# The low part of one weight unit, made later in VectorE's order

## The chip, the cores and the metric

One core of a Trainium2 chip runs the whole kernel. The metric is the device time of one execution in microseconds (us); three runs of the kernel before gave 766.83, 767.84 and 767.82 us, median 767.82.

## The reference

A two-layer decoder trunk on 256 tokens with 1024 features, in float32. Layer one is a stick-breaking attention with 16 heads of 64; layer two is a dilated windowed attention that reads a shared K/V. Each layer ends in a SwiGLU feed-forward. The change lies in layer one, at the end of its attention:

```python
z = jnp.einsum('bhqd,bhkd->bhqk', q_blk, kf) * scale
log_stay = jnp.where(strict, jax.nn.log_sigmoid(-z), 0.0)
log_a = jax.nn.log_sigmoid(z) + lax.cumsum(after, axis=3, reverse=True)   # after: log_stay moved on by one
a = jnp.where(strict, jnp.exp(log_a), 0.0)
o = jnp.einsum('bhqk,bhkd->bhqd', a, vf)      # all heads, then  o @ w_o
```

## The kernel before

Every engine has its own list of instructions, written out by hand, and runs it in that order; semaphores join the lists. No planner places anything: an instruction stands where the program puts it.

**Weights.** They pass through in units, numbered in one row over the whole program. A unit is loaded by SyncE's queue into one of three buffers `raw` (number modulo 3), its high part is made by ScalarE (`hi(s)`, line 511) and its low part, raw minus high, by VectorE (`lo(s)`, line 800), into six buffers `w_hi` and `w_lo`. TensorE then makes three matmuls for each product (high by high, high by low, low by high). The load of unit s waits for the low part of unit s - 3 (`sp.wait_ge(lo_made, ...)` in `load`), the high part for the landing, the low part for the high part. Units 20 and 21 are the query and key weights of head pair 7, the last one, of 1024 columns each. Units 22 to 25 are the four units of the first output projection (`WOA0` = 22), of 2048 columns; units 26 on are the feed-forward.

**Attention of layer one** goes by eight pairs of heads, 0 to 7. For a pair, VectorE takes the projected queries and keys out of PSUM (`take_qk_a`, lines 921 and 922); TensorE makes the scores (`scores_a`, lines 1252 and 1253); ScalarE makes three steps of a softplus (lines 579, 581, 583; the last signals `ell_made`); VectorE's `scores_a` makes four instructions (lines 900, 902, 903, 905) with ScalarE's line 593 between them; TensorE sums over the keys (`sums_a`, line 1285); VectorE subtracts that (`stay_a`, line 912); ScalarE's exponential (line 596) and VectorE's mask (`mask_a`, line 917) give the weights; TensorE multiplies them with the values (`outputs_a`, lines 1297 and 1299); VectorE cuts the output in two (`outputs_a`, lines 882 and 884). The pairs are staggered: while one pair is in its sums, the next one's projections run on TensorE.

**Around the change**, TensorE's list is: projections of pair 7 (lines 1197 to 1199, units 20 and 21), `sums_a(6)`, `scores_a(7)`, output projection by unit 22 and the first half of unit 23 (`out_proj`, lines 1191 to 1193), `outputs_a(6)`, more of it, `sums_a(7)`, unit 24, `outputs_a(7)`, the rest. VectorE's list is: take pair 6, stay 5, lo(20), mask 5, lo(21), lo(22), outputs 5, scores 6, take pair 7, stay 6, lo(23), mask 6, scores 7, outputs 6, lo(24), stay 7, lo(25), mask 7. SyncE's list there is: the load of unit 25 (which waits for lo(22)), four loads of x into `xn`, the load of unit 26 (which waits for lo(23)).

TensorE's `scores_a(7)` waits for `qka_made`, which the second instruction of `take_qk_a(7)` sends.

Of the kernel before, what the change touches and what calls it, by code (L numbers as in the profile page):

```python
# [34 lines left out]
PAIRS = NH // 2  # L35
# [26 lines left out]
WOA0 = A0 + 3 * PAIRS  # L62
# [39 lines left out]
def build(nc, x, norm_gains, w_qkv_a, w_o_a, g_kv, w_kv_b, w_q_b, w_o_b, rel_bias, w_gate_up, w_down,  # L102
# [16 lines left out]
    with ExitStack() as ctx:  # L119
# [94 lines left out]
        def bank(b, lo=0, n=512):  # L214
            return ps[:, 512 * b + lo:512 * b + lo + n]
# [5 lines left out]
        def banks(b, m, n):  # L221
            return ps[:, 512 * b:512 * (b + m)].rearrange("p (m n) -> p m n", m=m)[:, :, 0:n]
# [46 lines left out]
        def query_a(p):  # L269

            return A0 + (3 * p + 1 if p else 0)
# [5 lines left out]
        def size(s):  # L277
            return KT * P if s < WOA0 else 4 * NG * P if B0 <= s < WOB0 else UNIT
# [517 lines left out]
        def _(dve):  # L796
            def lo(s, j=0):
                dve.wait_ge(hi_made, j * 6 + s + 1)
                n, c = size(s), s % CUT
                dve.tensor_tensor(w_lo[:, c, 0:n], raw[:, s % RAW, 0:n], w_hi[:, c, 0:n].bitcast(F32), ALU.subtract  # L800
                                  ).then_inc(lo_made, 1)
# [84 lines left out]
            def outputs_a(a, j):  # L886

                dve.wait_ge(pva_done, j * 2 + a + 1)
                cut_ot(j * 2 + a, bank(7, 0, SEQ).rearrange("p (t m r) -> p t r m", t=NT, r=R), j * 2 + a + 1)

            def diagonals(buf):

                return buf.rearrange("p h (b n) -> p h b n", n=P)[:, :, 0:3:2, :]
# [3 lines left out]
            def scores_a(a, j):  # L897
                z = banks(3, 2, WA)
                dve.wait_ge(ell_made, j * 2 + a + 1)
                dve.scalar_tensor_tensor(spl, z, 0.0, ell, ALU.max, ALU.add).then_inc(spl_made, 1)  # L900
                dve.wait_ge(spl_made, j * 2 + a + 1)
                dve.tensor_tensor(diagonals(spl), diagonals(spl), strict4, ALU.mult).then_inc(spl_masked, 1)
                dve.scalar_tensor_tensor(arg, z, 0.0, ell, ALU.min, ALU.subtract).then_inc(arg_made, 1)
                dve.wait_ge(spl_hi, j * 2 + a + 1)
                dve.tensor_tensor(spl_cut[1], spl, spl_cut[0].bitcast(F32), ALU.subtract).then_inc(spl_cut_made, 1)

            def stay_a(a, j):
                dve.wait_ge(arg_made, j * 2 + a + 1)
                dve.wait_ge(r_done, j * 2 + a + 1)
                for lo_, n, b in ((0, SEQ, 5), (SEQ, P, 6)):  # L910
                    part = arg[:, :, lo_:lo_ + n]
                    inst = dve.tensor_tensor(part, part, two_heads(b, n), ALU.subtract)
                inst.then_inc(stay_made, 1)

            def mask_a(a, j):
                dve.wait_ge(wts_made, j * 2 + a + 1)
                dve.tensor_tensor(diagonals(wts), diagonals(wts), strict4, ALU.mult).then_inc(wts_masked, 1)

            def take_qk_a(p, j):
                dve.wait_ge(*((w_used, j * 6 + query_a(p) + 2) if p else (first_used, 2)))  # L920
                dve.scalar_tensor_tensor(qa, bank(0, 0, SEQ), SCALE, rows[:, :], ALU.mult, ALU.mult)
                dve.tensor_tensor(ka, bank(0, SEQ, SEQ), rows[:, :], ALU.mult).then_inc(qka_made, 1)

            def step_a(p, j):
                s = A0 + 3 * p + 4
                if p >= 2:
                    outputs_a(p - 2, j)
                scores_a(p - 1, j)
                take_qk_a(p, j)
                stay_a(p - 1, j)  # L930
                lo(s, j)
                mask_a(p - 1, j)
                lo(s + 1, j)
                lo(s + 2, j)


            rows2 = rows[:, :].rearrange("p (g n) -> p g n", g=1).broadcast_to([P, 2, SEQ])
# [181 lines left out]
            with dve.Fori(0, 2) as j:  # L1119
                step_a(2, j)  # L1120
                step_a(3, j)
            step_a(PAIRS - 2, 0)
            outputs_a(PAIRS - 3, 0)
            scores_a(PAIRS - 2, 0)
            take_qk_a(PAIRS - 1, 0)
            stay_a(PAIRS - 2, 0)
            lo(WOA0 + 1)
# [540 lines left out]
```

## Time and profile before

| | |
|---|---|
| median of three runs | 767.82 us |
| profiled execution, its own time | 767.52 us |
| its span, first to last instruction | 765.8 us |
| TensorE (PE) busy | 756.4 us, 99% |
| VectorE (DVE) busy | 495.1 us, 65% |
| ScalarE (ACT) busy | 418.2 us, 55% |
| GpSimd (POOL) busy | 175.4 us, 23% |
| mean granted TensorE clock | 0.998 of full |

The profile lists instructions with their start and duration in us from the start of the span. Engines take the next instruction shortly before the one at hand has ended, so the start to start distance of two neighbours (the pitch) is what counts in a sum, and it is a little less than a duration. The 1.7 us between span and time lie outside the program's instructions.

### The profile page before, as it was taken

To read this page: it belongs to the slowest core of one execution; us is meant where nothing else is said; L and a number is where in the kernel's file an instruction comes from. 1 tells how busy PE (TensorE), PEld (TensorE's weight loads), DVE (VectorE), ACT (ScalarE), POOL (GpSimd) and SP (SyncE) were. 2 spreads that over 40 slices of the span, in tenths; PEclk is the share of its full clock that TensorE was granted. 3 is DMA by queue.
4 is the path that set the end of the run, shared out by engine and by line. 5 is a ranking of instruction groups with operands and counts; after the bars stand their busy time and mean duration, and the time that the engine had idled before them with its cause. 6 is when DMAs were issued, how large, how long until landed. Compare 5 with 4: busy or idle time off the path is not lost.

```text
span 765.8 us, 13552 instructions
## 1 busy us (share of the span) xinstructions
PE 756.4 (99%) x4731; PEld 650.9 (85%) x4731; DVE 495.1 (65%) x676; ACT 418.2 (55%) x633; POOL 175.4 (23%) x299
## 2 busy tenths in 40 slices
PE   9999999999999999999999999999999999999996
PEld 7999978888888888999899899898888888888884
DVE  5888987775455455777766667668647745544543
ACT  4766668443343443865866766767655444333421
POOL 2000001660000000236654765557002000000000
PEclk9999999999999999999999999999999999999999
DMA  8744674896655554659586795796634765566402
GB/s 251 207 123 145 220 224 161 250 255 209 209 183 164 181 189 123 166 157 243 153 205 171 177 230 151 177 240 161 210 138 151 262 196 187 176 213 208 170 1 55
DMA packets 160259, 139.62 MB, mean 182 GB/s; under 512 B 8152, under 2 KB 149056, under 8 KB 160224
## 3 DMA queue, kind: packets, MB, share of 16 engines
q1 hardware_dynamic: 153248, 131.45, 55.8%
q0 software_dynamic: 6784, 7.41, 5.5%
q8 instruction: 21, 0.34, 0.2%
q10 hardware_dynamic: 192, 0.30, 0.2%
q14 instruction: 14, 0.11, 0.0%
HBM read 138.02 MB, written 1.11 MB: 182 GB/s over the span
## 4 chain that ended last, share of the span: by engine, by line
PE 96%; DMA 2%; ACT 1%; DVE 1%; issue 0%; SPq 0%; POOLq 0%; POOL 0%; DVEq 0%
PE ps L1191 20%; PE ps L1193 20%; PE ps L1192 20%; PE ps L1441 10%; PE ps L1443 5%; PE ps L1197 3%; PE ps L1199 3%; PE ps L1198 3%; PE ps L1355 1%; DMA raw<-in_w_o_b 1%; PE ps L1268 1%; PE ps L1285 1%; PE ps L1270 1%; PE ps L1504 1%; PE ps L1271 1%; PE ps L1243 1%
## 5 line engine op out<-in xcount | busy, mean ns | idle before, releaser
L800 DVE TENSOR_TENSOR w_lo<-raw,w_hi 128x2048 fp32r<-128x2048 f32 (+2 forms) x144 | 280.6, 1964 | 41.8 <-ACT w_hi L511 39.3
L511 ACT ACTIVATE w_hi<-raw 128x2048 fp32r<-128x2048 f32 (+2 forms) x144 | 232.7, 1637 | 58.3 <-DMA raw<-in_w_kv_b 28.0
L1191 PE MATMUL ps<-w_hi,xt 128*128 128x512 f32 x352 | 139.6, 397 | 0.0
L1193 PE MATMUL ps<-w_hi,xt 128*128 128x512 f32 x352 | 137.3, 390 | 0.0
L1192 PE MATMUL ps<-w_lo,xt 128*128 128x512 f32 x352 | 137.0, 389 | 0.0
L680 ACT ACTIVATE work<-ps,stat 128x256 f32<-128x256 f32 x44 | 21.0, 477 | 199.5 <-PE ps L1193 199.5
L422 POOL TENSOR_SCALAR stat<-stat 128x1 f32<-128x1 f32 x16 | 9.9, 617 | 440.0 <-ACT work L527 416.0
L1191 PE MATMUL ps<-w_hi,ot 128*128 128x512 f32 x240 | 94.9, 395 | 0.4 <-ACT work L641 0.4
L1193 PE MATMUL ps<-w_hi,ot 128*128 128x512 f32 x240 | 93.5, 390 | 0.0
L1192 PE MATMUL ps<-w_lo,ot 128*128 128x512 f32 x240 | 93.5, 390 | 0.0
L1193 PEld LDWEIGHTS ps<-w_hi,xt 128*128 128x128 f32 x352 | 66.0, 188 | 14.1
L1191 PEld LDWEIGHTS ps<-w_hi,xt 128*128 128x128 f32 x352 | 66.1, 188 | 13.5 <-issue 0.6
L1192 PEld LDWEIGHTS ps<-w_lo,xt 128*128 128x128 f32 x352 | 66.2, 188 | 12.8
L452 POOL DMA_DIRECT2D work<-bias_rows x128 | 71.2, 557 | 13.8 <-POOL work L471 9.1
L1045 DVE CAST ot<-ps 128x512 fp32r<-128x512 f32 x22 | 15.2, 692 | 77.0 <-PE ps L1355 77.0
L1191 PEld LDWEIGHTS ps<-w_hi,ot 128*128 128x128 f32 x240 | 45.0, 188 | 10.6 <-ACT work L641 0.8
L1193 PEld LDWEIGHTS ps<-w_hi,ot 128*128 128x128 f32 x240 | 45.0, 188 | 9.6
L1192 PEld LDWEIGHTS ps<-w_lo,ot 128*128 128x128 f32 x240 | 45.1, 188 | 8.9
L641 ACT ACTIVATE work<-ps,stat 32x128 f32<-32x128 f32 x128 | 45.8, 358 | 1.5
L469 POOL TENSOR_TENSOR work<-mask_b,work 128x128 f32<-128x128 bf16 (+1 forms) x32 | 26.3, 822 | 84.4 <-DMA work<-bias_rows 72.4
L1038 DVE SCALAR_TENSOR_TENSOR work<-ps,stat,work 128x256 f32<-128x256 f32 x44 | 21.1, 479 | 35.6 <-ACT work L680 35.6
L964 DVE TENSOR_TENSOR work<-ps,ob 128x256 f32<-128x256 f32 x42 | 17.7, 421 | 39.9 <-ACT ob L623 39.7
(148 smaller groups left out, 1325.3 us busy)
## 6 DMA issues: line engine op xcount, KB each, us to landing
raw<-in_w_gate_up SPq DMA_DIRECT2D x88, 512.0 KB, 4.9
raw<-in_w_kv_b SPq DMA_DIRECT2D x96, 256.0 KB, 4.3
raw<-in_w_down SPq DMA_DIRECT2D x22, 1024.0 KB, 5.0
raw<-in_w_q_b SPq DMA_DIRECT2D x48, 256.0 KB, 4.0
raw<-in_w_qkv_a SPq DMA_DIRECT2D x23, 512.0 KB, 5.0
raw<-in_w_o_a SPq DMA_DIRECT2D x4, 1024.0 KB, 6.4
work<-bias_rows POOLq DMA_DIRECT2D x128, 32.0 KB, 3.8
raw<-in_w_o_b SPq DMA_DIRECT2D x4, 1024.0 KB, 6.0
```

Of the source, the lines that this page charges most:

```text
L452: pool.dma_start(band[at_, t].rearrange("p (c n) -> p c n", c=R), bands[r][ds(h, 1)][:, :, t].rearrange("h m c n -> (h m) c n")).then_inc( ...
L469: pool.tensor_tensor(to[0], blocked[0], distances[:, 0:t + 1], ALU.add)
L511: act.activation(w_hi[:, s % CUT, 0:size(s)], raw[:, s % RAW, 0:size(s)], ACT.Copy).then_inc(hi_made, 1)
L641: inst = act.activation(vown[p % 2][row:row + HR, r], src[tokens, g], ACT.Copy, scale=x_rs(2, t)[tokens])
L800: dve.tensor_tensor(w_lo[:, c, 0:n], raw[:, s % RAW, 0:n], w_hi[:, c, 0:n].bitcast(F32), ALU.subtract).then_inc(lo_made, 1)
L1191: mm(out, xs[0], ws[0], start=start, stop=False)
L1192: mm(out, xs[0], ws[1], start=False, stop=False)
L1193: return mm(out, xs[1], ws[0], start=False, stop=stop)
L1197: mm(out, ws[0], xs[0], start=start, stop=False)
L1198: mm(out, ws[0], xs[1], start=False, stop=False)
L1441: mm(both, w[k // 4][0][:, k % 4, g, :], x_[:, :, k, :], start=k == 0, stop=False, skip_group_check=True)
L1443: inst = mm(bank(b, 0, SEQ), w[k // 4][1][:, k % 4, g, :], x_[:, 0, k, :], start=False, stop=k == KT - 1, skip_group_check=True)
```

## The change

`lo(22)` stood last in the step of pair 6. It is taken out of that step and put between VectorE's `scores_a` of pair 6 and its `take_qk_a` of pair 7. Nothing else is moved; the loops keep their three units.

```diff
-            def step_a(p, j):
+            def step_a(p, j, units=3):
...
                 stay_a(p - 1, j)
                 lo(s, j)
                 mask_a(p - 1, j)
-                lo(s + 1, j)
-                lo(s + 2, j)
+                for u in range(1, units):
+                    lo(s + u, j)
...
-            step_a(PAIRS - 2, 0)
+            step_a(PAIRS - 2, 0, 2)
             outputs_a(PAIRS - 3, 0)
             scores_a(PAIRS - 2, 0)
+            lo(WOA0)
             take_qk_a(PAIRS - 1, 0)
             stay_a(PAIRS - 2, 0)
             lo(WOA0 + 1)
```

## Rows read from the trace of the kernel before

**Rows 1.** The page: busy time, share and instructions of PE; the chain by engine.

```profile
PE 756.4 (99%) x4731; PEld 650.9 (85%) x4731; DVE 495.1 (65%) x676; ACT 418.2 (55%) x633; POOL 175.4 (23%) x299
...
PE 96%; DMA 2%; ACT 1%; DVE 1%; issue 0%; SPq 0%; POOLq 0%; POOL 0%; DVEq 0%
```

**Rows 2.** Waits of PE, whole span: who, for whom, us in total, times, longest.

```profile
PE ps L1551 <- DVE rows L1075: 1.3, 1, 1.3
PE ps L1191 <- ACT work L641: 0.4, 1, 0.4
```

**Rows 3.** Timeline of PE around the change: start, us, line, operation, count.

```profile
90.78 0.40 PE L1299 MATMUL ps<-work 128*64 128x128 f32 x4
...
96.83 0.28 PE L1199 MATMUL ps<-xt,w_lo 128*128 128x256 f32 x1
97.15 1.21 PE L1285 MATMUL ps<-xkv 128*128 128x512 f32 x6
98.29 0.71 PE L1252 MATMUL ps<-work 64*128 64x256 f32 x4
...
99.15 0.50 PE L1191 MATMUL ps<-w_hi,ot 128*128 128x512 f32 x1
...
102.01 0.39 PE L1191 MATMUL ps<-w_hi,ot 128*128 128x512 f32 x1
...
108.52 1.08 PE L1285 MATMUL ps<-xkv 128*128 128x512 f32 x6
109.54 0.50 PE L1191 MATMUL ps<-w_hi,ot 128*128 128x512 f32 x1
```

**Rows 4.** Timeline of DVE around the change; idle time before in brackets.

```profile
90.55 2.29 DVE L800 TENSOR_TENSOR w_lo<-raw,w_hi 128x2048 fp32r<-128x2048 f32 x1
92.75 0.42 DVE L882 CAST ot<-ps 128x256 fp32r<-128x256 f32 x1
...
93.55 0.95 DVE L900 SCALAR_TENSOR_TENSOR work<-ps,work 128x768 f32<-128x768 f32 x1
...
96.14 0.96 DVE L905 TENSOR_TENSOR xkv<-work,xkv 128x768 fp32r<-128x768 f32 x1
97.15 0.42 DVE L921 SCALAR_TENSOR_TENSOR work<-ps,rows 128x256 f32<-128x256 f32 x1
97.49 0.41 DVE L922 TENSOR_TENSOR work<-ps,rows 128x256 f32<-128x256 f32 x1
98.47 1.02 DVE L912 TENSOR_TENSOR work<-work,ps 128x512 f32<-128x512 f32 x2 [0.56 <-PE ps L1285]
99.40 2.29 DVE L800 TENSOR_TENSOR w_lo<-raw,w_hi 128x2048 fp32r<-128x2048 f32 x1
101.61 0.68 DVE L917 TENSOR_TENSOR work<-work 128x512 f32<-128x512 f32 x1
...
105.53 0.96 DVE L905 TENSOR_TENSOR xkv<-work,xkv 128x768 fp32r<-128x768 f32 x1
106.41 0.42 DVE L882 CAST ot<-ps 128x256 fp32r<-128x256 f32 x1
...
107.20 2.28 DVE L800 TENSOR_TENSOR w_lo<-raw,w_hi 128x2048 fp32r<-128x2048 f32 x1
```

**Rows 5.** Timeline of ACT around the change.

```profile
92.20 0.85 ACT L583 ACTIVATE work<-work 128x768 f32<-128x768 f32 x1
...
95.25 0.85 ACT L593 ACTIVATE xkv<-work 128x768 fp32r<-128x768 f32 x1 [1.48 <-DVE work L902]
96.01 3.69 ACT L511 ACTIVATE w_hi<-raw 128x2048 fp32r<-128x2048 f32 x2
```

**Rows 6.** DMA issues from 92 to 95 us: count, KB each, us to landing.

```profile
raw<-in_w_o_a SPq DMA_DIRECT2D x1, 1024.0 KB, 7.8
```

**Rows 7.** Stretches at the end: length, busy of five engines, PE's granted clock, DMA share, GB/s.

```profile
758.00:759.00 1.00, 0.35 (x2) 0.00 (x0) 0.67 (x2) 0.62 (x2) 0.00 (x0) 1.00 0.11 25
...
762.00:763.00 1.00, 0.00 (x0) 0.00 (x0) 0.00 (x0) 0.00 (x0) 0.00 (x0) 0.72 0.80 172
```

## The prediction

> **What bounds the kernel now.** I read the page first. Matmuls fill 99% of the span and the chain that ended last is 96% TensorE [rows 1], so what counts is whether TensorE is held up. The waits of TensorE over the whole span come next: there are only two, one in the first microseconds and one of 0.4 us far behind the change [rows 2]. So behind the change there is next to no idle time of TensorE that could swallow a delay: an idle microsecond given to it in layer one comes out at the end, unless it shortens that 0.4 us. Third I read the timelines of TensorE, VectorE and ScalarE around the change, each row against the row that it waits for.
>
> TensorE ends the projections of pair 7 and is ready for the sums of pair 6 at 96.83 + 0.12 = 96.95 (0.12 is the start to start distance of these matmuls, 0.28 their pipelined duration). It starts them at 97.15 [rows 3], 0.05 after VectorE's line 905 ended at 96.14 + 0.96 = 97.10 [rows 4]; that is the signal. So here VectorE is already a little late. Then scores of pair 7 at 98.29: their queries were ready at 97.49 + 0.41 = 97.90, so here TensorE is not held. From 99.15 the output projection runs [rows 3].
>
> **The change part by part.** It adds and removes no instruction. One subtraction of 2048 columns, pitch 92.75 - 90.55 = 2.20 (101.61 - 99.40 = 2.21 at its neighbour), goes from ahead of the output cut of pair 5 and the four instructions of pair 6's scores to behind them, ahead of the queries of pair 7 [rows 4].
>
> *What is taken away ahead of the scores.* VectorE is free at 90.55 in place of 92.75. The cut needs TensorE's outputs, ended at 90.78 + 0.40 = 91.18 [rows 3]; it starts at about 91.24 and takes a pitch of 93.55 - 92.75 = 0.80, so VectorE could begin line 900 at 92.04. Line 900 needs ScalarE's line 583, which ends at 92.20 + 0.85 = 93.05 [rows 5]; with 0.03 for the signal it starts at 93.08, where it started at 93.55 [rows 4]. The gain is 0.47 and not 2.2: ScalarE is late next. Line 593 of ScalarE was waiting for VectorE (1.48 idle, [rows 5]) and moves along, so line 905 starts at 96.14 - 0.47 = 95.67 and ends at 96.63, before TensorE asks at 96.95. The sums start at 96.95 unstalled; they take between 109.54 - 108.52 = 1.02, the next pair's, and 98.29 - 97.15 = 1.14, their own behind a stall [rows 3]. TensorE is ready for the scores of pair 7 at 97.97 to 98.09.
>
> *What is put ahead of the queries.* After line 905 the next VectorE instruction follows at a pitch of 106.41 - 105.53 = 0.88 [rows 4]: lo(22) from 95.67 + 0.88 = 96.55 to 98.76, its high part being made before 90.55. Behind it on VectorE stand `take_qk_a(7)`, `stay_a(6)` and lo(23). Lines 921 and 922 then take 0.34 + 0.41 = 0.75 [rows 4]: the queries are there at 99.51, the scores start at 99.56 in place of 98.29 [rows 3]. TensorE stands idle for some 1.6 us; the 0.2 lost at the sums before is gone. **Net: 99.56 - 98.29 = +1.27 us.** Refilling TensorE after the stall is bounded by 0 and 1.14 - 1.02 = 0.12; I take 0, since that is the nearer one: the scores came behind the sums' own end before and gain as much by finding the engine empty.
>
> *Does the rest move rigidly?* Each later need moves by 1.27; each supply must move by no more.
> - Unit 22 itself: made at 98.84, needed at 99.15 + 1.27 = 100.42. Hidden with 1.6 to spare.
> - `stay_a(6)` stood waiting 0.56 for the sums [rows 4]. Now the sums are over and it follows the queries at 99.44, so VectorE is late by 0.97 from here on. lo(23) runs from 100.37 to 102.66 and is needed at 102.01 + 1.27 = 103.28: cover 0.6, where 101.69 against 102.01 gave 0.3 [rows 3, 4].
> - lo(24) ended at 107.20 + 2.28 = 109.48, needed at 109.54, a cover of 0.06 [rows 3, 4]. It moves by 0.9 to 1.0 and the need by 1.27, so this thin cover grows. Were it to move more, each hundredth beyond would be paid.
> - DMA: the load of unit 25 is queued behind lo(22), so it is issued at 98.86 in place of 92.84, with the four loads of x behind it and unit 26 behind those. Unit 26 waited for lo(23) anyway, now at 102.66. Unit 25 landed in 7.8 us with other loads ahead of it [rows 6]; at 7.8 it lands at 106.7. VectorE wants its high part only behind `stay_a(7)`, which follows the next sums: 109.54 + 1.27 + a pitch of 0.93 = 111.7. A high part takes 3.69 / 2 = 1.85 [rows 5], so landings up to 109.9, or 11 us after the issue, cost nothing. x is read only in the update behind the whole output projection. The cost of the moved DMAs is put at 0; without that cover it is a microsecond for each microsecond beyond 11.
>
> Nothing more is gained elsewhere: ScalarE finishes line 593 and the two high parts 0.47 earlier [rows 5], but then waits for `stay_a(6)`.
>
> Could TensorE work past the stall? The output projection is ready to run and stands right behind the scores. Rows show it starting only after them [rows 3]; nothing in the list orders it ahead. The Trainium skill, "TensorE: Matmul & The Clock Gate", section "The mechanism", says that weight loads may be pulled ahead while matmuls start and end strictly in order. By that the stall is paid in full; if matmuls could pass, the sum would be about -0.3, the stall at the sums.
>
> **Sum.** 767.52 of the profiled execution + 1.27 = 768.8. The median of the runs shown is 0.30 above that execution, so the same step on it gives 767.82 + 1.27 = **769.1**, which I predict.
>
> **The rivals.**
> - *The front gain is lost.* If line 900 does not start earlier (ScalarE's three steps slip too), lo(22) starts at 97.02, the queries are there at 99.98, scores at 100.03: +1.74, with the refill of 0.12 +1.86, 769.6 to 769.7. Against it: VectorE's line 900 started 0.50 after its input was there [rows 4, 5].
> - *The other side: the queries are not late.* If VectorE had the queries by 97.92, TensorE would pay nothing and save the stall of the sums: 98.29 - 97.97 = 0.32 gained, 767.5. It decides at lo(22)'s start: before 97.92 - 0.75 - 2.21 = 94.96. For it speaks that VectorE is free from 92.04; against it that line 905 waits for ScalarE until 95.67 and the subtraction stands behind it. The change would have to do something else than the list says.
> - *The clock.* TensorE's last matmul ends at 758.35, and the granted clock leaves full, the 2.4 GHz level, only between 762 and 763, whose mean is 0.72 [rows 7]; so some 3.7 us idle passed without a loss, and the new gap is 1.6. Should it drop to 1.2 GHz there and stay for as long as those 3.7 us, matmuls at double length cost 1.8 more: +3.1, 770.9. The skill's page named above, section "Why this matters for your kernels", warns of idle gaps between bursts of matmuls dropping the clock; by the rows this gap is too short.
> - *The late load.* If unit 25 lands a microsecond beyond its cover, 770.1. Against it: it now has an empty queue ahead of it.
>
> **How the numbers follow.** Forecast 0.78 (own range 768.4 to 769.8: the sum with 0 to 0.12 of refill, and the 1.0 us over which three runs spread), lost front gain 0.09, other side 0.05, clock 0.04, load 0.04. The range 768.1 to 770.2 takes in the forecast, the lost gain and the load; it leaves out the other side and the clock. What a measurement can tell from no change is 0.2%, 1.54 us, and the forecast of 1.27 lies just inside it: I give it six to four on that side. So within: 0.78 x 0.6 + 0.03 of the other side + 0.02 of the lost gain, 0.52; slower: 0.78 x 0.4 + 0.07 + 0.04 + 0.04 of lost gain, clock and load, 0.46; faster 0.02, the rest of the other side.
>
> **What would show it.** In the profile after: line 900 of pair 6 at 93.08, sums at 96.95 without idle time ahead, a subtraction from 96.55 to 98.84, a new wait of TensorE for VectorE's line 922 of about 1.6 us, scores at 99.56, and from there every TensorE row later by 1.27 up to the end. The prediction is wrong if the scores start before 98.3 or after 100.0, if TensorE shows a second new wait before 126, or if the shift shrinks on the way to the end.

## The result and the profile after

The change takes 768.36 us, median of 22 executions (767.96 to 769.72); the kernel before, now with 22 executions, 767.17. Ratio 1.0014, 95% interval 1.0008 to 1.0020: slower by some 1.1 us, clear of no change, and inside the 0.2% that the prediction set as its bound. 769.1 was predicted, with a step of 1.27 on a median of 767.82 that came out 0.65 lower with more executions; the measured step between the medians is 1.19, and 1.03 in the second series below (768.17 against 767.14).

The profiled execution of after took 769.0 us with a span of 767.3 us. Its clock of instructions is later than that of before by 1.11 us from the head on (line 1199 of before at 96.83 is line 1200 of after at 97.94; lines behind the edit are one higher). That shift is there before the change is reached, so rows below are compared after taking 1.11 off.

TensorE's waits over the whole span, who, for whom, us in total, times, longest:

```profile
PE ps L1253 <- DVE work L922: 1.5, 1, 1.5
PE ps L1552 <- DVE rows L1075: 1.3, 1, 1.3
PE ps L1564 <- DMA xn<-in_x: 0.4, 1, 0.4
```

Against [rows 2] there is one new wait at the change, for the queries. The third line is a wait in the first microseconds, part of the 1.11 above, and the 0.4 us at 548 us is gone. TensorE's timeline there, to be read against [rows 3]:

```profile
97.94 0.28 PE L1200 MATMUL ps<-xt,w_lo 128*128 128x256 f32 x1
98.06 1.09 PE L1286 MATMUL ps<-xkv 128*128 128x512 f32 x6
100.66 0.71 PE L1253 MATMUL ps<-work 64*128 64x256 f32 x4 [1.51 <-DVE work L922]
101.20 0.40 PE L1254 MATMUL ps<-work 64*128 64x128 f32 x4
101.52 0.50 PE L1192 MATMUL ps<-w_hi,ot 128*128 128x512 f32 x1
...
110.93 1.09 PE L1286 MATMUL ps<-xkv 128*128 128x512 f32 x6
111.86 0.40 PE L1192 MATMUL ps<-w_hi,ot 128*128 128x512 f32 x1
```

The sums follow the projections without a pause (0.12, the pitch of the matmuls, where it was 0.32), and the scores stand for 1.51 us. VectorE's timeline, against [rows 4]:

```profile
92.33 0.42 DVE L882 CAST ot<-ps 128x256 fp32r<-128x256 f32 x1 [0.60 <-PE ps L1300]
...
94.18 0.96 DVE L900 SCALAR_TENSOR_TENSOR work<-ps,work 128x768 f32<-128x768 f32 x1 [0.96 <-ACT work L583]
...
96.78 0.96 DVE L905 TENSOR_TENSOR xkv<-work,xkv 128x768 fp32r<-128x768 f32 x1
97.66 2.29 DVE L800 TENSOR_TENSOR w_lo<-raw,w_hi 128x2048 fp32r<-128x2048 f32 x1
99.86 0.42 DVE L921 SCALAR_TENSOR_TENSOR work<-ps,rows 128x256 f32<-128x256 f32 x1
100.20 0.41 DVE L922 TENSOR_TENSOR work<-ps,rows 128x256 f32<-128x256 f32 x1
...
101.45 2.28 DVE L800 TENSOR_TENSOR w_lo<-raw,w_hi 128x2048 fp32r<-128x2048 f32 x1
...
109.17 2.28 DVE L800 TENSOR_TENSOR w_lo<-raw,w_hi 128x2048 fp32r<-128x2048 f32 x1
```

The time freed ahead of the scores is spent in two new pauses of VectorE, 0.60 for TensorE's outputs and 0.96 for ScalarE's line 583; the subtraction then stands whole in front of lines 921 and 922. The load of unit 25, issued here some 6 us later than before, landed in less time than in [rows 6], counted from its issue (columns: count, KB, us to landing):

```profile
raw<-in_w_o_a SPq DMA_DIRECT2D x1, 1024.0 KB, 5.0
```

TensorE's granted clock stayed at full through the hole (columns as in [rows 7], the clock is the third number from the end):

```profile
98.00:101.00 3.00, 1.49 (x12) 1.18 (x13) 3.00 (x4) 2.35 (x2) 0.00 (x0) 1.00 0.00 0
101.00:102.00 1.00, 1.00 (x10) 0.81 (x7) 1.00 (x3) 0.43 (x1) 0.00 (x0) 1.00 0.92 127
```

### The profile page after: what moved, and what is told of

Its sections match the earlier page's. It is cut to its first block, busy times and chain, and to the rows that moved or that the text cites. A ratio compares the mean times of both kernels' runs of the same rounds, so it can differ in the third digit from the quotient of the medians.

```text
span 767.3 us, 13552 instructions
## 1 busy us (share of the span) xinstructions
PE 756.6 (99%) x4731; PEld 651.9 (85%) x4731; DVE 495.2 (65%) x676; ACT 418.6 (55%) x633; POOL 176.2 (23%) x299
## 3 DMA queue, kind: packets, MB, share of 16 engines
HBM read 138.02 MB, written 1.11 MB: 181 GB/s over the span
## 4 chain that ended last, share of the span: by engine, by line
PE 97%; DVE 1%; ACT 1%; DMA 1%; issue 0%; POOLq 0%; SPq 0%; POOL 0%; DVEq 0%
PE ps L1192 21%; PE ps L1194 20%; PE ps L1193 20%; PE ps L1442 10%; PE ps L1444 5%; PE ps L1198 2%; PE ps L1200 2%; PE ps L1199 2%; PE ps L1356 1%; PE ps L1505 1%; PE ps L1244 1%; PE ps L1269 1%; PE ps L1470 1%; PE ps L1271 1%; PE ps L1272 1%; PE ps L1286 1%
## 5 line engine op out<-in xcount | busy, mean ns | idle before, releaser
L1442 PE MATMUL ps<-xkv,w_hi 128*128 128x512 f32 x168 | 43.3, 399 | 0.0
L1192 PE MATMUL ps<-w_hi,xkv 128*128 128x384 f32 x128 | 43.1, 337 | 0.0
```

The lines of the kernel that those rows point to most:

```text
L1192: mm(out, xs[0], ws[0], start=start, stop=False)
L1442: mm(both, w[k // 4][0][:, k % 4, g, :], x_[:, :, k, :], start=k == 0, stop=False, skip_group_check=True)
```

## The experiments

All distances in this table are read from TensorE's timeline in each kernel's profile, from the start of the last projection matmul of pair 7, so that the head does not count. "Update" is the first transpose of the updated x behind the output projection (line 1212 of before).

| kernel | sums | scores | output projection | update | us median (before beside it) | ratio, 95% interval |
|---|---|---|---|---|---|---|
| before, first profile | 0.32 | 1.46 | 2.32 | 26.16 | | |
| before again (e1) | 0.32 | 1.45 | 2.31 | 26.18 | 767.11 (767.14) | 0.9999, 0.9990 to 1.0008 |
| the change, first profile | 0.12 | 2.73 | 3.59 | 27.27 | 768.36 (767.17) | 1.0014, 1.0008 to 1.0020 |
| the change again (e2) | 0.12 | 2.73 | 3.59 | 27.27 | 768.17 (767.14) | 1.0014, 1.0005 to 1.0023 |
| extra idle subtraction (e3) | 0.32 | 3.26 | 4.12 | 29.39 | 769.60 (767.14) | 1.0028, 1.0019 to 1.0038 |
| late load (e7) | 0.31 | 1.45 | 2.31 | 26.55 | 767.16 (767.14) | 1.0000, 0.9991 to 1.0009 |
| 64 columns (e4) | 0.12 | 1.14 | 2.00 | 25.77 | 766.77 (767.23) | 0.9995, 0.9986 to 1.0004 |
| behind the queries (e5) | 0.12 | 1.14 | 3.33 | 27.67 | 768.68 (767.23) | 1.0018, 1.0009 to 1.0027 |
| split (e6) | 0.12 | 1.14 | 2.00 | 25.77 | 766.95 (767.23) | 0.9997, 0.9988 to 1.0006 |
| gap + 256 columns (e8) | 0.12 | 3.07 | 3.93 | 29.15 | 770.01 (767.40) | 1.0031, 1.0019 to 1.0043 |
| gap + 1024 columns (e9) | 0.12 | 3.86 | 4.72 | 29.97 | 771.03 (767.40) | 1.0049, 1.0035 to 1.0063 |

**Both kernels again (e1, e2)**, unchanged, for what varies by itself.

> The kernel before, unchanged. Every theory: ratio 1.000 within 0.001, and 2.3 us from the last projection matmul of pair 7 to the first matmul of the output projection (99.15 - 96.83). It is run for what varies by itself: in the profiles at hand the first transposes took 1.1 us longer after the change than before, and TensorE's wait of 0.4 us for ScalarE at 548 us is gone. If both are chance, this run shows other values for them than the first profile of before; if the wait at 548 is part of the kernel and the change removed it, it is here again.

> The change, unchanged. Every theory: ratio 1.0014 within 0.001, 3.6 us from the last projection matmul to the first of the output projection, a wait of 1.5 us of TensorE for VectorE's line 922. For the wait at 548 us: if the change removes it, it is missing here too; if it is chance, it may be here.

The distances at the change repeat to 0.01, those at the update to 0.02. The last projection matmul stood at 96.83 and 97.31 us in two profiles of one kernel, so the head varies by chance. TensorE's wait at 548 us, the second of [rows 2], is chance too; in the second profile of before only the wait in the head, the first microseconds, is left:

```profile
PE ps L1551 <- DVE rows L1075: 1.3, 1, 1.3
```

**An extra idle subtraction in the new place, lo(22) kept in the old one (e3).** The first theory against late loads.

```diff
...
             scores_a(PAIRS - 2, 0)
+            for half in range(2):
+                cols = slice(1024 * half, 1024 * half + 1024)
+                dve.tensor_tensor(idle_cols[half], w_lo[:, WOA0 % CUT, cols].bitcast(F32),
+                                  w_hi[:, WOA0 % CUT, cols].bitcast(F32), ALU.subtract)
             take_qk_a(PAIRS - 1, 0)
```

> The kernel before with lo(22) in its old place and an idle subtraction of 2 x 1024 columns, whose result nothing reads, in the new place. Theory (the queries of pair 7 stand behind the subtraction): line 905 starts at 96.14 as before, plus 0.88, plus 2 x 1.14, plus 0.75 and 0.05 puts the scores at 100.1 in place of 98.29: +1.8 us there, ratio 1.002; more than the change itself, since the 0.47 in front isn't gained. Rival (the loss comes from unit 25 and x being loaded 6 us later): these loads leave as before, so 0, ratio 1.000.

The scores came 1.80 later, as the theory has it, with the loads as before; "late loads" would have given 0. But the median moved by 2.46, more than 1.8. The profile shows why. TensorE's timeline, and its clock by stretches:

```profile
100.43 0.71 PE L1256 MATMUL ps<-work 64*128 64x256 f32 x4 [1.72 <-DVE work L923]
...
102.72 0.63 PE L1195 MATMUL ps<-w_hi,ot 128*128 128x512 f32 x1
103.14 0.63 PE L1196 MATMUL ps<-w_lo,ot 128*128 128x512 f32 x1
...
105.51 0.39 PE L1197 MATMUL ps<-w_hi,ot 128*128 128x512 f32 x1
105.74 0.40 PE L1195 MATMUL ps<-w_hi,ot 128*128 128x512 f32 x1
```

```profile
98.00:100.50 2.50, 0.78 (x7) 0.52 (x6) 2.50 (x5) 2.05 (x2) 0.00 (x0) 1.00 1.06 344
100.50:101.50 1.00, 1.00 (x9) 0.85 (x10) 1.00 (x3) 0.17 (x1) 0.00 (x0) 0.92 1.02 209
101.50:102.50 1.00, 1.00 (x3) 0.81 (x4) 1.00 (x1) 1.00 (x2) 0.00 (x0) 0.50 1.09 250
...
105.00:106.00 1.00, 1.00 (x6) 0.78 (x6) 0.96 (x2) 0.00 (x0) 0.00 (x0) 1.00 0.86 239
```

After a hole of 1.72 us the clock fell to the 1.2 GHz level (0.50) just as work had begun again; matmuls of the output projection then start 0.42 apart in place of 0.23, and at the update the delay is 3.21 in place of 1.8. It is not so in every execution: of ten, five took 768.61 to 769.13 us (mean clock 0.997 to 0.999), five 770.08 to 770.53 (0.994 to 0.995). The lower five stand on the mean 1.72 above the median of before, about what the late queries alone account for.

**The load of unit 25 held back, VectorE's order as before (e7).**

```diff
             for u in range(4):
+                if u == 3:
+                    sp.wait_ge(stay_made, PAIRS - 1)
                 two_rows(WOA0 + u, 0, wo_dram[0][:, 2 * u:2 * u + 2, :])
```

> The kernel before with the load of unit 25, and with it the four loads of x behind it, held back until the stay of pair 6 is made (99.5 in place of 92.84 us). VectorE's order is the old one. Theory (late queries): 0, ratio 1.000, since landings up to 11 us after the issue are covered. Rival (late loads): the loss of the change is here, +1.2 us, ratio 1.0014.

Ratio 1.0000: the rival is out as the cause. The profile does show an edge of the cover, a wait of 0.2 us of TensorE at the update of x, 0.37 late there:

```profile
PE ps L1214 <- DVE xn L853: 0.2, 1, 0.2
```

It does not begin with unit 25. ScalarE's timeline shows it waiting for the feed-forward's units, which stand behind unit 25 and x in the queue, and what the update needs of ScalarE and VectorE stands behind that in their lists:

```profile
114.89 1.91 ACT L513 ACTIVATE w_hi<-raw 128x2048 fp32r<-128x2048 f32 x1 [2.33 <-DMA raw<-in_w_gate_up]
117.87 1.92 ACT L513 ACTIVATE w_hi<-raw 128x2048 fp32r<-128x2048 f32 x1 [1.06 <-DMA raw<-in_w_gate_up]
```

The loads leave 0.6 us later here than in the change, and for needs that are not put off by 1.3.

**Only 64 columns in the new place (e4).**

```diff
...
-            lo(WOA0)
+            lo(WOA0, 0, slice(0, 64))
             take_qk_a(PAIRS - 1, 0)
```

The rest of unit 22's low part is left out: its columns hold an older unit's values or zeros set early in the kernel.

> The change, but lo(22) in its new place covers only the first 64 of 2048 columns (the low part of the rest is left as zeros or old values, set early in idle time). Theory: what is left is the gain in front alone: line 900 waits for ScalarE, 905 ends before TensorE asks, the sums start unstalled and the scores follow them without a wait: 2.0 to 2.1 us from the last projection matmul to the output projection in place of 2.32, so -0.2 to -0.3 us, ratio 0.9996. Rival (late loads): unit 25 is still issued some 4 us late, so most of the loss stays, ratio 1.001.

The gain in front by itself: sums unstalled, scores without a wait, output projection at 2.00 in place of 2.31 and the update at 25.77 in place of 26.18. The ratio of 0.9995 fits these 0.3 to 0.4 us, though its interval holds 1. The late load does not show.

**One place later, behind the queries (e5).**

```diff
-            lo(WOA0)
             take_qk_a(PAIRS - 1, 0)
+            lo(WOA0)
```

> The change with lo(22) one place later, behind the queries of pair 7 and ahead of the stay of pair 6. Theory: the scores are not late (start some 1.1 us after the last projection matmul), but the output projection needs unit 22 at about 2.0 us after it and lo(22) runs from 1.0 to 3.3 us after it; so TensorE waits for line 800 some 1.2 us, and lo(23) comes 0.2 late too: 3.4 to 3.6 us from the last projection matmul to the output projection, +1.0 to +1.3 us, ratio 1.0015. Rival (only the queries matter): 2.1 us, no loss, ratio 0.9997.

The scores are on time and the wait has moved to the weights themselves:

```profile
PE ps L1192 <- DVE w_lo L800: 1.3, 1, 1.3
```

No loss was what "only the queries matter" expected; 1.0018 it is. The 3.33 us are just below what the first theory expected, the 1.45 us between the medians above its 1.0 to 1.3: 1.02 is lost up to the output projection, and nearly half a microsecond more behind it, where the first matmul by unit 23 starts 0.50 behind its neighbour in place of 0.23: lo(23) is late in its turn. Between the front place and the output projection VectorE has no hole of 2.2 us: in both places tried there, TensorE waits for what stands last.

**Split, 1536 columns in the old place and 512 in the new (e6)**; only the second part signals.

```diff
...
             step_a(PAIRS - 2, 0, 2)
+            lo(WOA0, 0, slice(0, 1536), False)
             outputs_a(PAIRS - 3, 0)
             scores_a(PAIRS - 2, 0)
-            lo(WOA0)
+            lo(WOA0, 0, slice(1536, UNIT))
```

> lo(22) in two parts: 1536 columns in its old place, 512 columns in its new place. Theory: the first part takes 1.7 us and fits with the cut into the time until ScalarE's line 583 is done, the second takes 0.6 us and fits between line 905 and the end of the projections, for which the queries wait anyway; so the sums start unstalled and the queries are not late: 2.0 to 2.2 us from the last projection matmul to the output projection in place of 2.32, -0.1 to -0.3 us, ratio 0.9997, faster than both kernels by a margin that only the profile can tell. Rival (anything ahead of the queries is paid): +0.3 us, 2.6 us.

VectorE's and TensorE's timelines show the second part between line 907 (905 of before) and the queries, at the cost of nothing: TensorE waits nowhere.

```profile
95.85 0.96 DVE L907 TENSOR_TENSOR xkv<-work,xkv 128x768 fp32r<-128x768 f32 x1
96.73 0.68 DVE L801 TENSOR_TENSOR w_lo<-raw,w_hi 128x512 fp32r<-128x512 f32 x1
97.33 0.41 DVE L923 SCALAR_TENSOR_TENSOR work<-ps,rows 128x256 f32<-128x256 f32 x1
```

```profile
97.00 0.28 PE L1203 MATMUL ps<-xt,w_lo 128*128 128x256 f32 x1
97.12 1.09 PE L1289 MATMUL ps<-xkv 128*128 128x512 f32 x6
98.14 0.71 PE L1256 MATMUL ps<-work 64*128 64x256 f32 x4
```

It has all of the gain and none of the loss, 0.31 ahead of before at the output projection and 0.41 at the update; medians 766.95 against 767.23. That is the best version here, but its interval holds 1: only the profile tells it from before.

**A longer hole (e8, e9).** The change with 256 or 1024 idle columns behind lo(22), to see whether the clock follows the length of the hole.

```diff
...
             lo(WOA0)
+            dve.tensor_tensor(idle_cols[:, 0:256], w_lo[:, 21 % CUT, 0:256].bitcast(F32),
+                              w_hi[:, 21 % CUT, 0:256].bitcast(F32), ALU.subtract)
             take_qk_a(PAIRS - 1, 0)
```

> The change with an idle subtraction of 256 columns, whose result nothing reads, behind lo(22) and ahead of the queries. TensorE's gap ahead of the scores grows from 1.5 by a pitch of some 0.35 to 1.85 us. Theory A (a hole costs its length, nothing else): +0.35 to the change, so +1.45 to the kernel before, ratio 1.0019, all executions alike. Theory B (with a gap of 1.7 and more, the granted clock falls to 1.2 GHz in a part of the executions, as it did in the profile of the run with 2 x 1024 idle columns, where 3.4 us at that level followed): executions in two groups, 1.7 us apart, the later group with a mean clock of 0.994 to 0.995 in place of 0.997 to 0.999; median between 768.6 and 770.3.

> The same with 1024 idle columns: the gap grows by 1.14 to some 2.65 us. Theory A: +2.25 to the kernel before, ratio 1.0029, all executions alike with clock 0.997 to 0.999. Theory B: the group with the lower clock is larger than with 2 x 1024 idle columns (where it was 5 of 10) and the median lies at +3.9, ratio 1.005.

The profile of e8, then that of e9, TensorE's clock by stretches:

```profile
100.50:101.50 1.00, 1.00 (x9) 0.82 (x9) 1.00 (x3) 0.28 (x1) 0.00 (x0) 1.00 0.43 127
101.50:102.50 1.00, 1.00 (x5) 0.80 (x4) 1.00 (x1) 1.00 (x2) 0.00 (x0) 0.76 1.05 430
102.50:103.50 1.00, 1.00 (x4) 0.81 (x3) 1.00 (x2) 0.97 (x2) 0.00 (x0) 0.50 1.01 414
```

```profile
100.50:101.50 1.00, 0.00 (x0) 0.00 (x0) 1.00 (x4) 0.00 (x0) 0.00 (x0) 1.00 0.30 66
101.50:102.50 1.00, 0.92 (x9) 0.77 (x9) 1.00 (x4) 0.01 (x1) 0.00 (x0) 1.00 0.97 373
102.50:103.50 1.00, 1.00 (x5) 0.85 (x4) 1.00 (x1) 1.00 (x2) 0.00 (x0) 0.63 0.99 410
```

Theory A, that a hole costs its length and nothing else, falls; theory B, that the clock falls in a part of the executions, holds. By the length of the hole ahead of the scores:

| hole, us | kernel | executions | about 1.5 us above what the hole alone gives |
|---|---|---|---|
| 1.51 and 1.52 | the change, both series | 33, 767.92 to 769.72, mean clock 0.996 to 0.999 | none by the clock |
| 1.72 | e3 | 10 | 5 |
| 1.85 | e8 | 6: 768.74 and 768.92; 769.98 to 771.10 | 4 |
| 2.65 | e9 | 5, 770.78 to 772.01 | 5 |

One execution of each kernel has a clock by stretches; the others are sorted by their time and mean clock together. A mean of 0.996 stands in both groups, and two of the 33 (769.47 and 769.72) lie 1.3 to 1.4 above their medians with 0.998 and 0.997, so the counts are a reading, not the clock itself.

## Why the prediction was right, and where it was not

*The number.* The predicted 769.1 is 0.74 above the measured 768.36, and 0.65 of that is the base, a median of three executions that came out high. With the later base the same step gives 768.44. That the range, whose lower end is 768.1, still held the result owes something to its width.

*The gain in front, 0.47 at line 900.* Right: 94.18 - 1.11 = 93.07, against 93.08 said, and what ended the pause is ScalarE's line 583.

*The sums unstalled at 96.95.* Right: 98.06 - 1.11. e4 and e6 show what it is worth by itself: 0.31 at the output projection.

*Queries at 99.51, scores at 99.56, +1.27.* Right: 100.61 and 100.66 less 1.11 are 99.50 and 99.55; 2.73 - 1.46 in the table is 1.27. TensorE waits 1.51 by the profile, where some 1.6 was said; the difference is the pipelined end of the sums. The refill after the stall cost 0, as taken: 3.59 - 2.73 and 2.32 - 1.46 are both 0.86. e3 and e5 show that it is the order of VectorE's list, and which instruction is behind it decides only where TensorE waits.

*The rest moves rigidly.* Not quite, and by the prediction's own sign (a shift that shrinks on the way to the end) this part was wrong. The shift is 1.27 at the output projection, 1.30 at the sums of pair 7, and 1.10 at the update. lo(24) moved by less than the need, as said, but its thin cover of 0.06 was not put at a price. Before, then after:

```profile
109.54 0.50 PE L1191 MATMUL ps<-w_hi,ot 128*128 128x512 f32 x1
109.87 0.39 PE L1192 MATMUL ps<-w_lo,ot 128*128 128x512 f32 x1
```

```profile
111.86 0.40 PE L1192 MATMUL ps<-w_hi,ot 128*128 128x512 f32 x1
112.09 0.40 PE L1193 MATMUL ps<-w_lo,ot 128*128 128x512 f32 x1
```

In before, the first matmul of unit 24 stood 1.02 behind the sums' start [rows 3] and the next one 0.33 behind it; in after, 0.93 and 0.23. lo(24) now ends at 109.17 + 2.28 = 111.45, a cover of 0.41. A cover of 0.06 is hardly more than a signal takes here (0.05 from line 905 to the sums, by the prediction), so TensorE was most likely held by lo(24) already; 0.19 is what that had cost, and the change gives it back. The step is mis-sized by that, and the 1.19 and 1.03 between the medians lie on either side of the 1.10. What is left reaches the end: from the last projection matmul of pair 7 to the last matmul of the kernel it is 661.50 and 661.39 us in the two profiles of the change, 660.40 in the second of before (the first has the wait at 548 us besides), so 1.0 to 1.1.

*Late loads at 0.* Right for the change (e7, and the load landed in 5.0). The prediction looked for the edge at unit 25; in e7, with loads 0.6 us later and the needs unmoved, it came at the units behind it in the queue.

*The clock.* The rival did not happen, yet the reason given against it was wrong. From [rows 7] I read that some 3.7 us idle pass without a loss; but there the kernel ends and nothing shows what would have followed. That row shows when the clock left full, not how long a hole must last for it: in e3 the clock fell some 0.9 us after the hole had ended. In the hole at the change the clock fell in half of the executions at 1.72 us and in all at 2.65. The change's own hole of 1.5 was 0.2 short of the shortest at which it fell here; that much was luck. The price per fall was 1.45 between the two groups of e3 (means 770.31 and 768.86), where 1.8 was said. The rival's chance deserved more than 0.04: with the lost front gain, a hole of 1.72 as in e3, the step is 1.7 or 3.2 by chance, and the second lies outside the range on any of the medians. The Trainium skill, "TensorE: Matmul & The Clock Gate", section "Why this matters for your kernels", warns of idle gaps between bursts of matmuls, but of longer ones than any here; the runs show the fall after 1.72 already, and the measurement decides.

What stays open: why, at one length of hole, one execution falls and the next does not; no run here varies anything else.

## What to carry to other kernels

Where one engine is busy 99%, move work on another engine only into pauses that its timeline shows, and cut it to fit: 2.2 us of subtraction found no pause, 1.7 and 0.6 us found two. What an instruction is moved past gains only until its next supplier is late (0.47 of 2.2 here), what stands behind it pays in full. A hole on TensorE cost its length at 1.5 us; from 1.7 us on it cost in some or all executions some 1.5 us more for the clock, so a forecast for a hole of that size needs both cases.

## What the runs showed of the hardware

TensorE's granted clock fell to the 1.2 GHz level after a hole of as little as 1.72 us in a stream that was otherwise full, and it fell when matmuls were running again: in e3 the hole ended at 100.43, and the mean of 100.5 to 101.5 is still 0.92. After 1.51 us it stayed at full in the profile. While it was low, matmuls of 512 columns started 0.42 to 0.43 us apart in place of 0.23.
